# Expert stage of a two-layer transformer kernel: four raw weight buffers instead of two, a single buffer for the split down weights, passes of 2048 columns, and gathers that skip padding rows

## The reference, cut to what matters

```python
buf = jnp.zeros((R, D), x.dtype).at[dest].set(x[stok])   # tokens grouped by expert, padded to 128 rows
def run_block(args):
    xb, e = args                                          # 128 rows, one expert
    hid = jax.nn.silu(xb @ w_gate[e]) * (xb @ w_up[e])    # 1024 -> 256
    return hid @ w_down[e]                                # 256 -> 1024
out = lax.map(run_block, (buf.reshape(nblk, MOE_BLOCK, D), blk_e)).reshape(R, D)
y = jax.ops.segment_sum(out[dest] * sw[:, None].astype(out.dtype), stok, num_segments=T)
```

## Time and profile before

| | us |
|---|---|
| median of three runs | 3122.04 |
| profiled execution | 3119.75 |
| its span | 3117.8 |
| expert stage of layer 0, from the first gather issue to the last scatter issue | 1189.52 to 1725.50 |
| expert stage of layer 1, first gather issue at | 2591.86 |
| PE busy, share of the span | 86% |
| DVE, ACT, POOL busy | 56%, 40%, 23% |
| mean granted clock of PE | 0.936 of full speed |

### The profile page before, as it was taken

How to read it: one execution, slowest core, us unless ns; L and a number is a source line. 1 busy time by engine, 2 the same in 40 slices (tenths; PEclk the granted TensorE clock), 3 DMA queues, 4 the chain that set the end, 5 groups by cost and what they waited for, 6 DMA issues and landing times. The chain is left out here.

```text
span 3117.8 us, 48627 instructions
## 1 busy us (share of the span) xinstructions
PE 2673.4 (86%) x15109; PEld 2236.8 (72%) x15112; DVE 1747.1 (56%) x3154; ACT 1260.4 (40%) x2369; POOL 724.0 (23%) x923
## 2 busy tenths in 40 slices
PE   5999979997968947998898599799879947989997
PEld 4999958875847836777676488578658836767775
DVE  4222246665755665667765366588733354676664
ACT  3222132225841104556654222288611104675653
POOL 1000023321110002444343143211100002444433
PEclk9999989998988968999999799899979968999998
DMA  6111112215536516899997322222154415999995
GB/s 243 50 56 52 40 60 78 75 65 165 163 121 234 194 61 216 261 301 302 316 281 228 118 87 80 91 83 88 53 198 143 149 39 179 298 359 285 283 308 132
DMA packets 175389, 509.57 MB, mean 163 GB/s; under 512 B 53800, under 2 KB 81456, under 8 KB 150320
## 3 DMA queue, kind: packets, MB, share of 16 engines
q1 hardware_dynamic: 142480, 393.69, 34.7%
q0 software_dynamic: 32800, 114.51, 15.4%
HBM read 374.56 MB, written 133.56 MB: 163 GB/s over the span
## 5 line engine op out<-in xcount | busy, mean ns | idle before, releaser
L1700 DVE TENSOR_TENSOR moe_parts<-expert_w,moe_parts 128x1024 fp32r<-128x1024 f32 x384 | 452.3, 1221 | 238.4 <-ACT moe_parts L1649 234.9
L1582 PE MATMUL ps<-moe_parts,moe_xT 128*128 128x512 f32 x2232 | 551.6, 403 | 23.0 <-issue 16.0
L1582 PEld LDWEIGHTS ps<-moe_parts,moe_xT 128*128 128x128 f32 x2232 | 418.1, 191 | 125.3 <-issue 20.5
L1649 ACT ACTIVATE moe_parts<-expert_w 128x1024 fp32r<-128x1024 f32 x384 | 373.3, 1047 | 80.3 <-PEq L155 78.8
L1109 PE MATMUL ps<-out_w,out_catT 128*128 128x512 f32 x1344 | 322.4, 399 | 14.2 <-DVE out_w L1265 11.8
L560 PE MATMUL ps<-in_gate_w,in_gate_hnT 128*128 128x384 f32 (+1 forms) x1536 | 319.4, 367 | 7.4 <-DVE in_gate_w L679 7.4
L1582 PE MATMUL ps<-moe_parts,moe_hidT 128*128 128x512 f32 x1116 | 289.0, 408 | 26.9 <-DVE moe_hidT L1713 24.2
L560 PEld LDWEIGHTS ps<-in_gate_w,in_gate_hnT 128*128 128x128 f32 x1536 | 278.7, 190 | 37.4 <-issue 7.5
L1109 PEld LDWEIGHTS ps<-out_w,out_catT 128*128 128x128 f32 x1344 | 255.7, 192 | 69.4 <-DVE out_w L1265 12.6
L560 PE MATMUL ps<-in_qk_w,in_qk_hnT 128*128 128x512 f32 x1152 | 268.4, 394 | 9.2 <-DVE in_qk_w L679 9.2
L1582 PEld LDWEIGHTS ps<-moe_parts,moe_hidT 128*128 128x128 f32 x1116 | 205.7, 191 | 76.2 <-DVE moe_hidT L1713 32.8
(11 more groups left out here) (262 smaller groups left out, 4150.8 us busy)
## 6 DMA issues: line engine op xcount, KB each, us to landing
expert_w<-in_w_gate SPq DMA_DIRECT2D x64, 1024.0 KB
expert_w<-in_w_up SPq DMA_DIRECT2D x64, 1024.0 KB
expert_w<-in_w_down SPq DMA_DIRECT2D x64, 1024.0 KB
hn_d<-out_hn SPq DMA_DIRECT2D x32, 512.0 KB, 2.6
in_gate_xt<-in_x SPq DMA_DIRECT2D x16, 512.0 KB
in_qk_xt<-in_x SPq DMA_DIRECT2D x16, 512.0 KB
att_k<-k_d SPq DMA_DIRECT2D x64, 128.0 KB, 2.9
out_ht<-in_x SPq DMA_DIRECT2D x16, 512.0 KB, 4.6
```

The lines of the kernel that those rows point to most:

```text
L1582: last = nc.tensor.matmul(out, left[:, a, k, :], right(b, k), start=(n == 0 and k == 0), stop=(n == 2 and k == K_ - 1))
L1649: nc.scalar.activation(parts[:, j, 0, at], K.expert_w[:, j, at], ACT.Copy).then_inc(w_high.sem, 1)
L1700: nc.vector.tensor_tensor(parts[:, j, 1, at], K.expert_w[:, j, at], parts[:, j, 0, at].bitcast(F32), ALU.subtract).then_inc(w_low.sem, 1)
```

## The change

The raw weights get a ring of four slots: the two of `expert_w` and two in a new tile `more`. The split gate and up weights stay double-buffered (`gu_parts`). The split down weights get one buffer (`d_parts`), so an expert's down weights are now split in its own first block and no longer in that of the expert before it. Passes are 2048 columns wide: two for gate and up, one for down. Experts are unrolled in fours. The gather takes its row numbers from the table `K.where`, in which a padding row has a number above 2047, and has a bounds check that skips such rows; `xg` is cleared once at the stage's start. ACT reads the gate values from the table itself. The load of `w_in_odd` waits for expert 29's splits instead of expert 31's.

```diff
-            self.expert_in = [[... for i in range(2)]
+            self.expert_in = [[... for i in range(RING)]
...
-    PIECE = 1024
+    PIECE = 2048
...
-        parts = sb("parts", [P, 2, 2, EW], F32R)
+        more = sb("more", [P, RING - 2, EW])
+        ring = [K.expert_w[:, i, :] for i in range(2)] + [more[:, i, :] for i in range(RING - 2)]
+        gu_parts = sb("gu_parts", [P, 2, 2, GU], F32R)
+        d_parts = sb("d_parts", [P, 2, EW - GU], F32R)
...
         def _(sp):
             def load(i, j):
-                load_expert(K, sp, layer, i * 2 + j, j, lambda n: alone(
-                    sp, w_low, i * (2 * PIECES) + ((j - 2) * PIECES + (n + 1) * PIECES // 3), K.tick_sp))
+                load_expert(K, sp, layer, i * RING + j, ring[j], K.expert_in[layer][j], lambda n: alone(
+                    sp, (Count(gu_low), Count(gu_low), Count(d_low))[n],
+                    ((i - 1) * RING + j) * (GU_PIECES, GU_PIECES, D_PIECES)[n] + (GU_PIECES // 2, GU_PIECES, D_PIECES)[n], K.tick_sp))
+            for j in range(2, RING):
+                load_expert(K, sp, layer, j, ring[j], K.expert_in[layer][j])
...
-                sp.wait_ge(w_low.sem, NE * PIECES)
+                sp.wait_ge(gu_low, (NE - RING + 2) * GU_PIECES)
+                sp.wait_ge(d_low, (NE - RING + 2) * D_PIECES)
                 sp.dma_start(K.w_in_odd, ...)
...
         def _(g):
-                nc.gpsimd.tensor_copy(who[:, :], K.who[:, m:m + 1] ...)
+                nc.gpsimd.tensor_copy(who[:, :], K.where[:, m:m + 1] ...)
                 nc.gpsimd.indirect_dma_start(xg[:, :], None, K.hn_d[layer],
-                                             bass.IndirectOffsetOnAxis(ap=who[:, :], axis=0)).then_inc(gathered_s, 16)
-            def set_gate(m):
-                nc.gpsimd.tensor_copy(gate[:, :], K.gates[:, bass.ds(m, 1)]).then_inc(gated.sem, 1)
+                                             bass.IndirectOffsetOnAxis(ap=who[:, :], axis=0),
+                                             bounds_check=T - 1, oob_is_err=False).then_inc(gathered_s, 16)
+            g.memset(xg[:, :], 0.0).then_inc(cleared, 1)
+            g.wait_ge(cleared, 1)
             gather(0)
...
         def _(pe):
                 if behind:
-                    lower(m - 1, 1 - j)
-                pe.wait_ge(w_low.sem, i * (2 * PIECES) + (j + 1) * PIECES)
+                    pe.wait_ge(d_low, i * (RING * D_PIECES) + j * D_PIECES)
+                    lower(m - 1)
...
         def _(a):
             def y_scaled(m):
                 until(a, down, m + 1)
-                until(a, gated, m + 1)
                 a.wait_ge(scattered_s, m * 16 + 16)
-                nc.scalar.activation(y[:, :], yp, ACT.Copy, scale=gate[:, 0:1]).then_inc(y_out.sem, 1)
+                nc.scalar.activation(y[:, :], yp, ACT.Copy, scale=K.gates[:, bass.ds(m, 1)]).then_inc(y_out.sem, 1)
             def first_block(i, j, m, behind, ahead):
                 if ahead:
-                    a.wait_ge(K.expert_in[layer][nj], ni * 48 + 48)
                     if behind:
                         until(a, up, m)
-                    split(ni, nj, range(GU_PIECES))
+                    split_gu(i + (j + 1) // RING, (j + 1) % RING)
                 act(m)
                 x_out(m + 1)
                 if behind:
                     y_scaled(m - 1)
-                if ahead:
-                    split(ni, nj, range(GU_PIECES, PIECES))
+                    split_d(j)
```

More of the change, by code:

```diff
@@ L1283, in _, with load_expert @@
             log(end.plus(1))
-def load_expert(K, sp, layer, e, slot, until_free=lambda n: None):
+def load_expert(K, sp, layer, e, dst, there, until_free=lambda n: None):
     nc = K.nc
@@ L1297, in load_expert @@
     src = src[e] if isinstance(e, int) else src[bass.ds(e, 1)].rearrange("a p n -> (a p) n")
[L1298 removed]
+    sp.dma_start(dst[:, DK * 2 * FF:], src).then_inc(there, 16)
 def route(K, layer):
@@ L1501, in in_turn, with round_ @@
         def in_turn(eng, first_block, block):
-            def pair(i, is_first, is_last):
-                for j in range(2):
-                    e = i * 2 + j
+            def round_(i, is_first, is_last):
+                for j in range(RING):
+                    e = i * RING + j
                     m0 = 0 if is_first and j == 0 else end_of(eng, e)
-                    first_block(i, j, m0, not (is_first and j == 0), not (is_last and j == 1))
+                    first_block(i, j, m0, not (is_first and j == 0), not (is_last and j == RING - 1))
                     end = end_of(eng, e + 1)
@@ L1643, in _, with split_gu, split_d @@
             a.sem_inc(y_out.sem, y_out.credit)
-            def split(i, j, pieces):
-                for n in pieces:
+            def split_gu(i, j):
+                a.wait_ge(K.expert_in[layer][j], i * 48 + 48)
+                for n in range(GU_PIECES):
                     at = slice(n * PIECE, (n + 1) * PIECE)
-                    nc.scalar.activation(parts[:, j, 0, at], K.expert_w[:, j, at], ACT.Copy).then_inc(w_high.sem, 1)
+                    nc.scalar.activation(gu_parts[:, j % 2, 0, at], ring[j][:, at], ACT.Copy).then_inc(gu_high, 1)
+            def split_d(j):
+                for n in range(D_PIECES):
+                    at = slice(n * PIECE, (n + 1) * PIECE)
+                    nc.scalar.activation(d_parts[:, 0, at], ring[j][:, GU + n * PIECE:GU + (n + 1) * PIECE], ACT.Copy).then_inc(d_high, 1)
             def x_out(m):
@@ L1684, in block_ @@
                 y_scaled(m - 1)
-            a.wait_ge(K.expert_in[layer][0], 48)
-            split(0, 0, range(PIECES))
+            split_gu(0, 0)
             x_out(0)
+            split_d(0)
             in_turn(a, first_block, block_)
```

85 lines of the change are left out of this document (43 added, 42 removed).

## The result

The changed kernel takes 3172.1 us (median of 4 runs, 3167.9 to 3183.7); the kernel before took 3122.3 beside it (3121.5 to 3127.5). The ratio is 1.0162, 95% interval [1.0132, 1.0191]: 50 us slower, where 3101 was forecast and 3140 was the upper end of the range. The profiled execution is the fastest of the four: 3167.88 us, span 3166.2, mean granted clock 0.928 (before 0.936).

A forecast was written before the change was run, and what follows sets the result against it. PE, busy about nine tenths of the expert stages, was taken as the bound, with only short waits to win. Forecast: 3119.75 - 26 + 0 + 11 - 6 = 3098.75, or 3101 on the median's scale; range 3068 to 3140.

The forecast's parts named there:

- The gather behind the burst: Two-block experts: the gather for the second block, queued behind three loads, counted as just in time, at 0.
- nothing moves: Rival: the burst holds the other gather back as much as it frees the first one; 3127, chance 0.13.
- The second blocks' gathers: Gather issued in an expert's second block finds nothing queued; the 1.22 us wait goes, block falls from 10.92 to 9.84.
- The -26: Gathers in two-block experts: 29 second blocks at 0.9 us each; ends -40 and +20.
- One-block experts: 35 experts: +6 for some 20 in succession, -7 for some 15 after two-block experts; together 0, ends +30 and -17.
- the slower rival: Wider passes cost more than the gathers give, since DVE starts later in nearly every first block; +34, 3156, chance 0.21.
- The start: Start of each stage: clearing xg and a gather behind six loads, 5.5 us per layer, +11; ends +9 and +26.
- The queue part: Stage start: six loads, 6 MB, queued before the first gather is issued, taken as 4.4 us.
- The clearing: Stage start: POOL's clearing of xg, like the memset of 0.95 us, 1.1 with its wait.
- The end of layer 0: Nonexistent block's gather skipped, saving PE's 8.91 us; 3 given back for the 5 MB load: -6, ends -9 and +3.
- The steps at nothing: Expert stages: POOL's gate copy gone, ACT's scale from the table (at worst +18), PE's down-pass wait, four slots: all 0.
- Turn-taking: Rival: queued loads do not hold a gather back; the start costs some 2 us instead of 5.5; 3094, chance 0.08.

## Why the prediction was wrong

**The gather behind the burst** is the step that failed. The prediction gave it "7.2 us from issue to use" and said: "I count it as just in time", because it holds 25 rows of 128. It takes 8.97 us, and the gather with no rows at all takes 14.85 us behind 5 MB. I had read from the earlier trace rows that the time depends on what SP has queued ahead, applied it to the gather that is relieved, and dropped it for the one that is loaded. The 0 of this step measures 20 us, 0.7 in each of 28 first blocks. And the step was missing where it counts as much: in one-block experts the burst stands ahead of the gather too, and spreading the loads gives 21 us back there. With second blocks that then grow, the net of it all is the 35 us between the two medians. The rival "nothing moves" had the right mechanism and priced it as a draw. It is no draw: besides PE's wait, an idle PE can cost slower products (the 93 down products take 304.2 us in all instead of 289.0, though the undisturbed one is shorter).

**The second blocks' gathers**: the 1.22 us wait goes where it was said to, the block is 9.50 instead of 9.84, at this place even better than forecast. On average second blocks gain nothing (11.2 us before and after): 8 of 28 last 12.5 us or more, before it were 3. The -26 was too large to begin with. Its 0.9 us a block came from one wait of 1.22, while all 28 second blocks of the kernel before wait 14.1 us for gathers. Of these 11.2 are gone, and their waits for hidden rows rose by 14.6.

**One-block experts**: "together 0", ends +30 and -17. They go from 10.80 to 11.62 us, +27 for 33 of them. The 0.85 us of ACT's longer pass was seen, as was the slower rival with this very place. What was missing is first the burst: PE's wait for gathers in these blocks goes from 13.9 to 29.3 us, that for hidden rows from 8.7 to 19.0. Second, the clock: in the case shown, 1.94 us of idle PE were followed by a product of 4.57 us instead of 3.01, and the mean down product here went from 3.01 to 3.23. The rival's cause, wide passes, is not it in the changed kernel, where narrow ones leave the waits for hidden rows at 53.0 us. With the loads spread and the first ones later the wide passes cost 14 us, with the burst 2.5; in the kernel before they gain. The size of this term thus depends on the rest of the schedule.

**The start**: 5.5 per layer forecast, 7.3 measured. The queue part, 4.4, measures 4.3. The clearing was 1.1 and is 3.0, since the first gather's issue rose from 1.12 to 2.84 us. But taking the queue part away gave nothing back in the whole time, so as a term of a sum it was worth less than its size.

**The end of layer 0**: -6 forecast. PE's 8.91 us became 6.90 for a real gather, and the last three blocks together take 38.0 us instead of 37.7. Worth nothing, and in the kernel before nothing could be gained there either.

**The steps at nothing**: nothing speaks against four buffers at 0, though no run has them alone. The shorter products stood in no term. The gate from the table measures 3 us, at the edge of the interval and within its bound of 18. PE's wait for the down pass is not visible apart.

**Turn-taking.** The prediction set the rule of the Trainium skill ("DMA: Bandwidth & Descriptors", section "Queues, rings and completion order") against the trace. From 1309 us on the trace agrees with it: q0 and q1 move packets in the same microseconds. From 1306.42 to 1309.11 the loads have the engines to themselves; whether the gather had a packet to send by then no row shows, so this part speaks neither for the rule nor against it. A gather beside three loads still takes 9 us where one beside a single load took 5.2. The forecast made beside the rule, 3094, was off by 78 us.

## What to carry to other kernels

When a change regroups transfers, ask of every latency-bound transfer behind the group, scatters too, how many bytes stand ahead when its packets arrive, not when it is issued and not how many bytes it has itself. Spread bulk loads over the period in which they are wanted rather than issuing them together; holding them back behind one small transfer only puts them ahead of the next. When one wait is shortened, look which one ends last in its place: here the time moved from the gather to the hidden rows. And price an idle time of PE near 2 us with the slower product that can follow it.

## What the runs showed of the hardware

- A gather with all rows out of range and nothing to fetch is not free: issued 1698.53, used 1713.38 behind 5 MB.
- A skipped row is still a packet: from 1269.40 to 1273.50 us in the changed kernel, when the gather of 50 rows arrives, its queue moves 154 packets but only 0.25 MB, and 117 of all packets of the window are under 512 bytes.
- A gather's first packet starts 1.8 us after its issue on POOL with nothing queued and 3.9 to 4.4 beside loads issued just behind it; that of a plain load 1.0 us after its issue.
- The issue of a gather on POOL takes 1.0 us, up to 1.93 beside DVE passes of 1024 columns (2.08 in the changed kernel with such passes) and up to 3.0 beside those of 2048. The source view of the changed kernel's line (ns, least, median, most):

```profile
L1541 POOL DMA_INDIRECT moe_xg<-hn_d,moe_who x97: 1009/1063/3006, 1186.8 to 3142.5; - x97
```

- PE's granted clock was 0.64 over a product that followed 1.94 us of idle time, and the product took 4.57 us instead of 3.01. After 1.50 us in the earlier trace rows it took 3.06.
